# Row sums of squares as two rounded products in the third tile of a stage, and the first two weight tiles split in halves

## The reference

```python
def rmsnorm(x, g):
    xf = x.astype(jnp.float32)
    y = xf * lax.rsqrt(jnp.mean(xf * xf, axis=-1, keepdims=True) + EPS)
    return (y * g.astype(jnp.float32)).astype(x.dtype)

for i in range(DEPTH):
    ...
    x = x + y.astype(x.dtype)
    x = x + sqrelu_mlp(rms_norm(x, norm_ffn[i]), ffn_w1[i], ffn_w2[i]).astype(x.dtype)
```

## Time and profile before

| | us |
|---|---|
| median of 3 runs | 1545.35 (1545.01 to 1547.52) |
| the profiled execution, its own time | 1544.95 |
| its span, from first to last instruction | 1543.2 |

### The profile page before, as it was taken

How to read it: one execution, slowest core, us unless ns; L and a number is a source line. 1 busy time by engine, 2 the same in 40 slices (tenths; PEclk the granted TensorE clock), 3 DMA queues, 4 the chain that set the end, 5 groups by cost and what they waited for, 6 DMA issues and landing times.

```text
span 1543.2 us, 34873 instructions
## 1 busy us (share of the span) xinstructions
PE 1531.6 (99%) x12812; PEld 1494.0 (97%) x12812; DVE 1044.8 (68%) x1764; ACT 849.2 (55%) x1300; POOL 122.4 (8%) x123
## 2 busy tenths in 40 slices
PE   9999999999999999999999999999999999999999
PEld 8899999988999999999999999999999998999999
DVE  7777765644876657666787766668576657787764
ACT  6776654536665445555445555556555547665543
POOL 1830000045000000000000000000000033200000
PEclk9999999999999999999999999999999999999999
DMA  7146656554666665556565655656566971066564
GB/s 254 62 132 196 192 190 203 165 173 142 193 193 200 189 196 191 191 192 204 190 207 193 200 191 191 208 182 210 189 194 193 235 213 61 16 204 192 193 201 151
DMA packets 80640, 280.53 MB, mean 182 GB/s; under 512 B 8864, under 2 KB 12448, under 8 KB 80544
## 3 DMA queue, kind: packets, MB, share of 16 engines
q1 hardware_dynamic: 76656, 274.29, 55.0%
q10 hardware_dynamic: 3888, 4.85, 1.7%
HBM read 277.53 MB, written 1.57 MB: 181 GB/s over the span
## 4 chain that ended last, share of the span: by engine, by line
PE 94%; DVE 4%; ACT 1%; issue 1%; DMA 0%; SPq 0%; ACTq 0%; DVEq 0%
PE psum L1776 27%; PE psum L1777 27%; PE psum L1780 27%; PE psum L1918 2%; PE psum L1920 2%; PE psum L1919 2%; PE psum L2209 1%; PE psum L2160 1%; DVE w_lo L1052 1%; PE psum L2105 0%; PE psum L1983 0%; PE psum L2193 0%; PE psum L1973 0%; DVE scratch L1649 0%; ACT w_hi L578 0%
## 5 line engine op out<-in xcount | busy, mean ns | idle before, releaser
L578 ACT ACTIVATE w_hi<-raw 128x1024 fp32r<-128x1024 f32 x517 | 546.1, 1058 | 475.9 <-PE psum L1780 432.5
L1052 DVE TENSOR_TENSOR w_lo<-raw,w_hi 128x1024 fp32r<-128x1024 f32 x482 | 589.3, 1223 | 253.7 <-ACT w_hi L578 253.4
L1776 PE MATMUL psum<-xs,w_hi 128*128 128x256 f32 x1904 | 528.5, 278 | 0.5 <-DVE w_lo L1052 0.4
L1777 PE MATMUL psum<-xs,w_hi 128*128 128x256 f32 x1904 | 526.0, 276 | 0.0
L1780 PE MATMUL psum<-xs,w_lo 128*128 128x256 f32 x1904 | 526.0, 276 | 0.0
L1776 PEld LDWEIGHTS psum<-xs,w_hi 128*128 128x128 f32 x1904 | 357.4, 188 | 1.1 <-DVE w_lo L1052 0.9
L1777 PEld LDWEIGHTS psum<-xs,w_hi 128*128 128x128 f32 x1904 | 357.4, 188 | 0.2
L1780 PEld LDWEIGHTS psum<-xs,w_lo 128*128 128x128 f32 x1904 | 357.3, 188 | 0.0
L1780 PE MATMUL psum<-hs,w_lo 128*128 128x256 f32 x1280 | 353.3, 276 | 0.0
L1776 PE MATMUL psum<-hs,w_hi 128*128 128x256 f32 x1280 | 353.3, 276 | 0.0
L1777 PE MATMUL psum<-hs,w_hi 128*128 128x256 f32 x1280 | 353.3, 276 | 0.0
(11 more groups left out here) (292 smaller groups left out, 1482.8 us busy)
## 6 DMA issues: line engine op xcount, KB each, us to landing
raw<-tiles SPq DMA_DIRECT2D x517, 512.0 KB, 4.2
bias<-bias_dram ACTq DMA_DIRECT2D x8, 256.0 KB, 7.4
x<-x_in SPq DMA_DIRECT2D x4, 256.0 KB, 5.2
w1c_all<-w1c_k ACTq DMA_DIRECT2D x4, 256.0 KB, 4.2
w1c_all<-w1c_v ACTq DMA_DIRECT2D x4, 256.0 KB, 5.9
y_out<-x SPq DMA_DIRECT2D x8, 128.0 KB, 2.3
con<-consts SPq DMA_DIRECT2D x1, 803.0 KB, 9.0
bias_dram<-bias_row ACTq DMA_DIRECT2D x1, 512.0 KB, 7.1
```

The lines of the kernel that those rows point to most:

```text
L578: act.activation(slot_part(w_hi[s], t + RING * q if isinstance(q, int) else t), raw[s][:, :], ACT.Copy).then_inc(hi_ready, 1)
L1052: dve.tensor_tensor(slot_part(w_lo[s], t_), raw[s][:, :], hi_of(slot_part(w_hi[s], t_)), ALU.subtract).then_inc(lo_ready, 1)
L1776: pe.matmul(out, w_hi[s][:, c:c + P], x_hi, start=first, stop=False)
L1777: pe.matmul(out, w_hi[s][:, c:c + P], x_lo, start=False, stop=False)
```

## The change

1. At the seven stages `up_0`, mgate, `up_1`, `glu_0`, cin, `glu_1`, `glu_3` and at `kv` the sum over partitions is no longer one float32 matmul. ACT rounds `ssq` into the first half of a new buffer `ssq_parts` and DVE writes the rest into its second half; PE multiplies both with `ones_r`, ones in fp32r: two matmuls of the stream's own shape and type. `ssq_parts` lies over the first words of `scratch`, 16 words in; `ones_r` is a new buffer.
2. In the seven stages the sums move from the last chunk of `two()` to the third chunk of tile 2. At `kv` they stay in the middle of the first group.
3. The `odd_matmul` behind `two()` goes; at mgate alone (norm `mix_1`, in `TO_COLUMNS`) one stands behind tile 2.
4. The start: x's first two quarters are issued on ACT's queue, tile 0 is loaded in two halves, and tiles 0 and 1 are split and waited for in halves; 15 instead of 24 matmuls on ones.
5. In bytes of a partition: the weights `w_hi`, `w_lo` begin at multiples of 128, and `xs`, `os`, `hs` 64 past a multiple, before and after. `ones` begins 64 past, `ssq` 96 past (32 after the change), the weights of `odd_matmul` 32 past. `ones_r` begins at a multiple of 128 and the used part of `ssq_parts` 64 past one. `ssq`, `std`, `rb`, `kT`, `vtok`, `kcT`, `vc` move up by 576 bytes, `os`, `xs`, `hs` and `arena` by 512.

```diff
+        with nc.sbuf_tensor("ssq_parts", [P, 16 + 2 * S], F32R) as ssq_parts:
+            ssq_parts = ssq_parts[:, 16:]
         scratch = sb("scratch", [P, 12 * S])
...
+        sb("apart_r", [P, 16])
+        ones_r = sb("ones_r", [P, P], F32R)
...
-        sb("apart", [P, 120])
+        sb("apart", [P, 104])
...
-            sp.dma_start(raw[0][:, :], tiles[0]).then_inc(tile_loaded[0], 16)
-            for j in range(1, 4):
+            sp.dma_start(raw[0][:, 0:TILE // 2], tiles[0][:, 0:TILE // 2]).then_inc(first_half, 16)
+            sp.dma_start(raw[0][:, TILE // 2:], tiles[0][:, TILE // 2:]).then_inc(tile_loaded[0], 16)
+            for j in range(2, 4):
...
             def root(name):
+                if name in TO_ROWS and name != "mix_0":
+                    act.wait_ge(ssq_ready, SSQ0[name] + KD + 1)
+                    act.activation(ssq_parts[:, 0:S], ssq[:, :], ACT.Copy).then_inc(ssq_split, 1)
                 act.wait_ge(stat_done, STAT0[name])
...
+            for j in range(2):
+                act.dma_start(x[:, 2 * j * S:2 * (j + 1) * S], x_in[:, 2 * j * S:2 * (j + 1) * S]).then_inc(x_loaded[j], 16)
             act.preload_act_table(ACT.Copy)
...
             def norm(name):
+                if name in TO_ROWS and name != "mix_0":
+                    hi, lo = ssq_parts[:, 0:S], ssq_parts[:, S:]
+                    dve.wait_ge(ssq_split, 2 * TO_ROWS.index(name) - 1)
+                    dve.tensor_tensor(lo, ssq[:, :], hi_of(hi), ALU.subtract).then_inc(ssq_split, 1)
                 dve.wait_ge(std_ready, STD0[name])
...
                     if name in TO_ROWS:
-                        ins = pe.matmul(bank(RB, 0, S), ones[:, :], ssq[:, :], start=True, stop=True)
+                        if name == "mix_0":
+                            ins = pe.matmul(bank(RB, 0, S), ones[:, :], ssq[:, :], start=True, stop=True)
+                        else:
+                            pe.wait_ge(ssq_split, 2 * TO_ROWS.index(name))
+                            pe.matmul(bank(RB, 0, S), ones_r[:, :], ssq_parts[:, 0:S], start=True, stop=False)
+                            ins = pe.matmul(bank(RB, 0, S), ones_r[:, :], ssq_parts[:, S:], start=False, stop=True)
...
                     for k in range(KD):
                         if wait_x:
                             pe.wait_ge(xs_ready, XS0[xs_name] + k + 1)
+                        if paired and isinstance(i, int) and (u + 4 * i, k) == (2, 2):
+                            sums(norm_)
...
                         pe.wait_ge(xs_ready, XS0[xs_name] + k + 1)
-                        if norm_ and k == KD - 1:
-                            sums(norm_)
...
-                if odd:
-                    odd_matmul()
                 for u in range(2 if paired else 0, head):
                     one(u, 0, u == 0)
+                    if odd and u == 2 and norm_ in TO_COLUMNS:
+                        odd_matmul()
...
-            warm(24)
+            warm(15)
```

More of the change, by code:

```diff
@@ L226, in build @@
         hi_ready, lo_ready = sem("hi_ready"), sem("lo_ready")
+        first_half, half_hi, half_lo = sem("first_half"), sem("half_hi"), sem("half_lo")
         tile_done = sem("tile_done")
@@ L971, in nsa, with split_half @@
                 out_hi("o_n")
+            for j in range(2):
+                act.dma_start(x[:, 2 * j * S:2 * (j + 1) * S], x_in[:, 2 * j * S:2 * (j + 1) * S]).then_inc(x_loaded[j], 16)
             act.preload_act_table(ACT.Copy)
+            def split_half(t, n):
+                cols = slice(n * TILE // 2, (n + 1) * TILE // 2)
+                if (t, n) == (0, 0):
+                    act.wait_ge(first_half, 16)
+                else:
+                    act.wait_ge(tile_loaded[t], 16)
+                act.activation(w_hi[t][:, cols], raw[t][:, cols], ACT.Copy).then_inc(half_hi if n == 0 else hi_ready, 1)
             act.wait_ge(vec_loaded, 16)
@@ L980, in _ @@
                 if k == 1:
-                    split(0)
-            split(1)
+                    split_half(0, 0)
+                if k == 3:
+                    split_half(0, 1)
+            split_half(1, 0)
+            split_half(1, 1)
             for k in range(KD):
@@ L1708, in nsa, with take_half @@
                 out_lo("o_n", range(2, KD))
+            def take_half(t, n):
+                cols = slice(n * TILE // 2, (n + 1) * TILE // 2)
+                dve.wait_ge(half_hi if n == 0 else hi_ready, t + 1)
+                dve.tensor_tensor(w_lo[t][:, cols], raw[t][:, cols], hi_of(w_hi[t][:, cols]), ALU.subtract)\
+                   .then_inc(half_lo if n == 0 else lo_ready, 1)
+            dve.wait_ge(const_ready, 1)
+            dve.tensor_copy(ones_r[:, :], ones[:, :])
             dve.wait_ge(vec_loaded, 16)
@@ L1715, in _ @@
                 if k == 1:
-                    take_lo(0)
-            take_lo(1)
+                    take_half(0, 0)
+                if k == 3:
+                    take_half(0, 1)
+            take_half(1, 0)
+            take_half(1, 1)
             def squares(chunks, others, out=None):
@@ L1817, in one @@
                     s, b = (t0 + u) % RING, 7 if side else (o0 + u) % 4
-                    pe.wait_ge(lo_ready, i * 4 + (t0 + u + 1))
+                    halves = isinstance(i, int) and t0 + u + 4 * i < 2
+                    if halves:
+                        pe.wait_ge(half_lo, t0 + u + 1)
+                    else:
+                        pe.wait_ge(lo_ready, i * 4 + (t0 + u + 1))
                     if not side and not (isinstance(i, int) and o0 + u + 4 * i < 4):
@@ L1823, in one @@
                             pe.wait_ge(xs_ready, XS0[xs_name] + k + 1)
+                        if paired and isinstance(i, int) and (u + 4 * i, k) == (2, 2):
+                            sums(norm_)
+                        if halves and k == KD // 2:
+                            pe.wait_ge(lo_ready, t0 + u + 1)
                         if t0 + u in PACKED:
```

4 lines of the change are left out of this document (2 added, 2 removed).

## The result

| | us |
|---|---|
| changed kernel, median of 4 runs | 1580.15 (1580.0 to 1582.8) |
| kernel before, beside it | 1546.03 (1545.0 to 1547.5) |
| ratio | 1.0227 (1.0214 to 1.0239) |

The prediction was 1543.3, with a range up to 1546.3. It was wrong by 37 us. The page of the changed kernel shows little of the cause: PE is as busy as before, and longer. The one sign of it is the mean duration of a stream matmul, 279 ns on line 1814 where line 1777 had 276.

What follows compares the result with a forecast made beforehand. PE, busy 99% of the span, was taken to bound the kernel. Sums -2.73, waits +0.04, +0.43 and +0.79, kv -0.20, start -0.40 give -2.07 us: 1543.3 us, range 1540.9 to 1546.3.

Steps and rivals of the forecast that it cites:

- tile 4 waits: Tile 4 waits for DVE's later split: +0.04 us for up_0 and up_1 together, +0.43 at cin, none at glu stages.
- rival 3: Short pitch lost at one place, by waits in cin, up_0, up_1 or after wo_n: 1548 to 1553 us, chance 0.10.
- rival 2: The new products break the pitch, so all that follows in the six stages is long: about 1580 us, chance 0.09.
- glu_1 and glu_3 alike: At glu_0 tile 4's slack of 1.79 us exceeds the 1.68 needed, so no wait; glu_1 and glu_3 the same.
- a finished split reaches PE in 0.06 us: Time from the end of DVE's split to PE's start, part of the 1.68 us slack that tile 4 needs.
- no longer repairs the pitch at a stage's start: Argument for the short pitch being lost at one place: without the odd matmul, PE cannot restore it when a stage begins.
- the odd matmul failed: In mgate, behind the column sums, the odd matmul did not restore the short pitch; long pitch assumed, 0.55 us kept for range.
- The sums: Two products replace float32 sum and odd matmul in six stages: gain 0.455 us a stage, -2.73 us in all.
- kv: Two products (0.23 us) replace the old sum (0.43 us) on the chain that ended last: -0.20 us.
- The start: Earlier x and half tiles: PE's first matmul near 7.4, gain between 0 and 0.9 us, taken as -0.40 us.
- mgate: Root 1.16 us later, so tile 4 starts at 304.90 instead of 304.11: +0.79 us, a wait of about 1.1.
- Buffers moved: nothing: Moved buffers, 15 warming matmuls and ones_r cost nothing, since the stream's operands keep their place modulo 128 bytes.

Runs made afterwards that it cites:

- the fastest version: Changed kernel with the sum at the first chunk of tile 2, at cin one matmul later: 1542.03 us, ratio to the kernel before 0.9981.

## Why the prediction was wrong, point by point

- **The step that failed** is "tile 4 waits", as rival 3 put it: "A wait in the middle of the short pitch hasn't been seen". The sum priced up_0's and up_1's waits at 0.04 us together, their own length, and cin's at 0.43. Their own length was priced too low: the weight loads of up_0 and up_1 came 0.12 us late each, 0.25 together. (cin's row came 0.24 late in a stage entered long, where PE reaches tile 4 later by the 42 matmuls since the new products, 42 x 4.5 ns = 0.19; together that is the 0.43.) But the length hardly matters: each of the first two turned the pitch for the rest of its stage and what follows, up_0's up to mgate and up_1's up to `kv`, from where the kernel before was long too. The price that the sum lacked is the number of matmuls behind the wait times 4.5 ns: at glu_1, measured alone, 6.65 us. Rival 3 had the mechanism at one stage (1548 to 1553); it struck at every place it could, which gave rival 2's time (1580) without rival 2's mechanism.
- **glu_3** had no wait in the sum, "glu_1 and glu_3 alike". Its weight load was 45 ns late there: the split ended at 1400.02, 0.19 ahead of tile 4's first row, and that was not enough. glu_0 and glu_1, once entered short (the run with three odd matmuls in tile 7), had 0.17 and were 0.07 late. The term that was too small is "a finished split reaches PE in 0.06 us". It was read where PE stood waiting (and holds so at up_0, 127.51 to 127.57); in the stream the weight load starts 0.11 us ahead of its matmul, so the split must end earlier by at least as much. At cin in the fastest version 0.20 was enough. A margin under 0.2 us should have counted as a wait.
- **That PE "no longer repairs the pitch at a stage's start"** was named under rival 3, and right. But the odd matmul is a repair only where it falls 118 or 119 ns behind its neighbour; in a short stretch it is the thing that lengthens. And mgate, where the prediction read that "the odd matmul failed", is entered long in five traces with the old sums, and there the column sums and the odd matmul led back in all five.
- **The sums.** Predicted -2.73. In up_0 of the kernel before the sum, the odd matmul and the 8 stream matmuls among them take 1593 ns, 8 x 113.3 = 907 of it the stream's; two products take 227. That is 0.46 a stage, -2.75 for six. Right.
- **kv.** Predicted -0.20. From kv's first matmul to kvc's first it is 23.37 us before (1023.38 to 1046.76) and 23.17 in the fastest version (1020.47 to 1043.64). Right.
- **The start.** Predicted -0.40. PE's first stream matmul is at 7.62 (8.77 before), tile 2 at 14.38, and wo_a's first odd matmul is 0.65 earlier. ACT's first split of x came at 4.95 against 5.22. Two traces don't size it, though. Over the 15 traces with the new start and the 5 with the old one, the attention's first matmul (uk) is at 26.96 (26.70 to 27.19) and 27.52 (27.26 to 27.76) on average, and ACT's first split at 5.01 and 5.18. So the start gives some 0.55 us, inside its bounds, and 0.17 of it is the earlier `x`. That the rest comes from the halves is not shown by a run.

```profile
4.95 0.91 ACT L600 ACTIVATE xs<-x,vec 128x256 fp32r<-128x256 f32 x2 [1.98 <-DMA x<-x_in]
```

- **mgate.** Predicted a wait of about 1.1: PE's tile 4 starts 1.15 behind its neighbour, so 1.03 late, with the split's end:

```profile
309.37 0.28 PE L1817 MATMUL psum<-xs,w_lo 128*128 128x256 f32 x1
310.52 0.39 PE L1813 MATMUL psum<-xs,w_hi 128*128 128x256 f32 x1 [0.87 <-DVE w_lo L1074]
```

  Right, and gone to 0.33 with the sum two chunks earlier.
- **"Buffers moved: nothing"** held for the fastest version, which has the same buffers and all six stages short, and was wrong as a statement on buffers: with the old sums kept, ssq alone at another address costs 37 us. The cover I named (the stream's operands keep their place modulo 128) left ssq out.
- With all stages short the prediction's terms hold: 1543.3 was forecast for the change as made. The fastest version has mgate's wait smaller by 0.70 and none of cin's 0.43, which makes 1542.2, and took 1542.0.

The Trainium skill ("TensorE: Matmul & The Clock Gate", "Back-to-back issue gap") has one isolated gap for a shape, and for a stream of weight loads and matmuls one spacing each for 128 and for 512 columns. Every trace here has two for 256 columns, 113.3 and 117.8 ns at the same granted clock of 1.0, for the same instructions on the same buffers; by a rule with one value for a shape none of the 37 us would exist.

## What to carry to other kernels

Where one engine is busy 99% of the span, look first at the distance of its instructions per stage, and price a wait not by its length but by what it does to the stream behind it: a weight load 0.12 us late cost 6.4 us in one window here (18 products x 3 x 117.8 ns). Read such a wait from the weight loads (PEld): the matmul's own row showed 15 ns of it. Leave 0.2 us or more at every place where the stream could wait, and compute the margin with the stream at its fast pitch. A repair such as the odd matmul held for one layout here; when a change touches a buffer that it reads or an instruction ahead of it, try that alone.

## What the runs showed of the hardware

- A weight load that comes late in the stream, the shortest seen by 42 ns, is followed by a pitch of 117.8 instead of 113.3 ns in 19 of 20 cases, for as long as nothing but the stream follows, over 170 us and more. 170 ns at glu_1 cost 6.65 us in a run that changed nothing else. In the program's first 15 us a wait was also followed by the short pitch, in six traces.
- A float32 matmul of 60 columns in the short stretch does the same, 46 times of 46. Three in one tile, placed as in wo_a, led back 64 times of 64.
- The address of a float32 matmul's moving operand, at 32, 160 or 224 instead of 96 modulo 256 bytes, shifts the start of what follows by 2 ns (305 instead of 307), and costs 37 us by way of the odd matmul. What in the chip makes the two pitches no run shows.
